# Laying the low parts of weights, x and activations 64 bytes further on in a decoder trunk

## The reference

```python
h = h + 0.5 * swiglu(rmsnorm(h, ln_ffn1[i]), ffn1_wi[i], ffn1_wo[i])   # d_ff = 2816
u = rmsnorm(h, ln_mix[i])
h = h + mixer(u)                     # layers 0 and 3: stick-breaking attention, 1: mLSTM, 2: latent attention
h = h + 0.5 * swiglu(rmsnorm(h, ln_ffn2[i]), ffn2_wi[i], ffn2_wo[i])
# swiglu(x, wi, wo): gate, up = split(x @ wi); (silu(gate) * up) @ wo
```

## Time and profile before

| | |
|---|---|
| time, median of 3 runs (lowest to highest) | 1944.04 us (1943.8 to 1944.66) |
| time of the profiled execution | 1943.6 us |
| its span, first to last instruction | 1941.9 us |
| its mean granted TensorE clock | 0.998 of full speed (2.4 GHz) |
| PE busy | 1922.5 us, 99% of the span, 10778 matmuls |
| PEld busy | 1657.6 us, 85% |
| DVE busy | 1367.0 us, 70% |
| ACT busy | 1128.4 us, 58% |
| DMA | 343.35 MB, mean 177 GB/s |

### The profile page before, as it was taken

The page is one execution under the profiler, slowest core; times in us unless marked ns, Lnnn a source line. Parts: engine busy times, 40 slices in busy tenths (PEclk is TensorE's granted clock), DMA queues, the critical chain, the costliest instruction groups (busy, mean ns, idle before and its releaser), DMA issues.

```text
span 1941.9 us, 29533 instructions
## 1 busy us (share of the span) xinstructions
PE 1922.5 (99%) x10778; PEld 1657.6 (85%) x10778; DVE 1367.0 (70%) x1844; ACT 1128.4 (58%) x1678; POOL 64.3 (3%) x138
## 2 busy tenths in 40 slices
PE   8999999999999999999999999999999999999998
PEld 6888988888888888888888889888888888978887
DVE  6766776767776686676777776676677776767666
ACT  6555575555655566655565555765555556556553
POOL 2000000000100000000010001000000000000000
PEclk9999999999999999999999999999999999999999
DMA  6555534655555553455655554355556555535553
GB/s 219 194 194 196 174 131 137 210 194 193 165 192 190 170 195 130 154 194 194 208 175 192 186 172 124 130 174 194 194 173 204 186 185 178 172 125 166 192 194 119
DMA packets 244095, 343.35 MB, mean 177 GB/s; under 512 B 12077, under 2 KB 196026, under 8 KB 244026
## 3 DMA queue, kind: packets, MB, share of 16 engines
q1 hardware_dynamic: 242016, 340.29, 53.1%
q10 hardware_dynamic: 2010, 2.12, 0.5%
HBM read 340.27 MB, written 1.05 MB: 176 GB/s over the span
## 4 chain that ended last, share of the span: by engine, by line
PE 95%; DVE 2%; ACT 1%; DMA 0%; issue 0%; SPq 0%; ACTq 0%; POOL 0%; POOLq 0%; DVEq 0%
PE psum L532 33%; PE psum L695 33%; PE psum L703 17%; PE psum L990 5%; PE psum L563 1%; PE psum L1634 1%; DVE wlo L494 1%; PE psum L1032 1%; ACT whi L475 0%; PE psum L1691 0%; DVE mix L1181 0%; DMA raw<-in_ffn_wi 0%; PE psum L1043 0%; PE psum L1721 0%; PE psum L1668 0%
## 5 line engine op out<-in xcount | busy, mean ns | idle before, releaser
L475 ACT ACTIVATE whi<-raw,gains 128x512 fp32r<-128x512 f32 (+2 forms) x876 | 557.1, 709 | 266.5 <-PE psum L703 192.7
L695 PE MATMUL psum<-xT,whi 128*128 128x512 f32 x2816 | 678.6, 392 | 2.3 <-DVE wlo L515 1.9
L494 DVE SCALAR_TENSOR_TENSOR wlo<-raw,gains,whi 128x512 fp32r<-128x512 f32 (+2 forms) x876 | 596.8, 743 | 57.5 <-ACT whi L475 57.5
L695 PEld LDWEIGHTS psum<-xT,whi 128*128 128x128 f32 x2816 | 522.5, 188 | 111.2 <-issue 4.8
L703 PEld LDWEIGHTS psum<-xT,wlo 128*128 128x128 f32 x2816 | 344.3, 189 | 6.8
L703 PE MATMUL psum<-xT,wlo 128*128 128x256 f32 x2816 | 346.3, 281 | 0.0
L811 DVE TENSOR_TENSOR gate_in_T<-psum,low 128x512 f32<-128x512 f32 x88 | 60.9, 692 | 337.8 <-ACT low L758 337.4
L490 DVE TENSOR_TENSOR wlo<-raw,whi 128x2048 fp32r<-128x2048 f32 x100 | 228.5, 2285 | 43.7 <-ACT whi L471 43.7
L532 PE MATMUL psum<-wlo,hidT_hi 128*128 128x512 f32 x640 | 251.4, 393 | 0.0
L532 PE MATMUL psum<-whi,hidT_hi 128*128 128x512 f32 x640 | 249.0, 389 | 0.0
L532 PE MATMUL psum<-whi,hidT_lo 128*128 128x512 f32 x640 | 248.6, 388 | 0.0
(11 more groups left out here) (230 smaller groups left out, 1534.5 us busy)
## 6 DMA issues: line engine op xcount, KB each, us to landing
raw<-in_ffn_wi SPq DMA_DIRECT2D x350, 512.0 KB, 4.6
raw<-in_ffn_wo SPq DMA_DIRECT2D x176, 512.0 KB, 4.3
raw<-in_sb_w_in SPq DMA_DIRECT2D x48, 512.0 KB, 4.5
raw<-in_ml_w_in SPq DMA_DIRECT2D x24, 512.0 KB, 4.4
raw<-in_sb_w_out SPq DMA_DIRECT2D x16, 512.0 KB, 4.0
raw<-in_ml_w_out SPq DMA_DIRECT2D x8, 512.0 KB, 4.0
raw<-in_mla_w_out SPq DMA_DIRECT2D x8, 512.0 KB, 4.3
raw<-in_mla_w_in SPq DMA_DIRECT2D x4, 512.0 KB, 4.5
```

Of the source, the lines that this page charges most:

```text
L475: last = act.activation(whi[:, slot, r], raw[:, slot, r], ACT.Copy, scale=gain_col(p.gain + k))
L494: last = dve.scalar_tensor_tensor(wlo[:, slot, p.at + r.start:p.at + r.stop], raw[:, slot, r], gain_col(p.gain + k), hi[:, r], op0=ALU.mul ...
L695: i = pe.matmul(psum[:, 4 + blk, :], whi[:, slot, k * 2 * FC + blk * P:k * 2 * FC + (blk + 1) * P], xT[:, 4 * part + k, :, :].rearrange("p ...
```

## The change

The diff moves tiles; no instruction is added or removed on any engine. Beside what is shown, only the order of declarations changes.

```diff
-                  for s in range(2)], at=SHIFT)
+                  for s in range(2)])
...
         whi = sb("whi", [P, RING, PCOLS], F32R)
-        wlo = sb("wlo", [P, RING, PCOLS + 32], F32R)
+        minus_half = sb("minus_half", [P, 16])
+        wlo = sb("wlo", [P, RING, PCOLS], F32R)
+        gains1 = sb("gains1", [P, N_GAINS_1])
         ssq = sb("ssq", [P, TT])
         mean_sq = sb("mean_sq", [P, TT])
...
         h = sb("h", [P, TT, D])
-        xT = sb("xT", [P, KD, 2, SEQ], F32R)
-        xT_hi, xT_lo = xT[:, :, 0, :], xT[:, :, 1, :]
+        hidT_hi = sb("hidT_hi", [P, FC // P, SEQ], F32R)
+        xT = sb("xT", [P, 2, KD * SEQ + 16], F32R)
+        xT_hi, xT_lo = (xT[:, a, 0:KD * SEQ].rearrange("p (k n) -> p k n", k=KD) for a in range(2))
+        gains2 = sb("gains2", [P, N_GAINS_2])
+        ident_b = sb("ident_b", [P, P], BF16)
+        hidT_lo = sb("hidT_lo", [P, FC // P, SEQ], F32R)
         hid = sb("hid", [P, 2, SEQ])
...
-                dve.tensor_tensor(wlo[:, slot, p.at:p.at + w], raw[:, slot, 0:w], hi[:, 0:w], ALU.subtract).then_inc(lo_ready, 1)
+                dve.tensor_tensor(wlo[:, slot, 0:w], raw[:, slot, 0:w], hi[:, 0:w], ALU.subtract).then_inc(lo_ready, 1)
...
-                i = pe.matmul(psum[:, 4 + blk, :], whi[:, slot, k * 2 * FC + blk * P:k * 2 * FC + (blk + 1) * P],
-                              xT[:, 4 * part + k, :, :].rearrange("p a n -> p (a n)"),
+                i = pe.matmul(psum[:, 4 + blk, :].rearrange("p (a n) -> p a n", a=2), whi[:, slot, k * 2 * FC + blk * P:k * 2 * FC + (blk + 1) * P],
+                              xT[:, :, (4 * part + k) * SEQ:(4 * part + k + 1) * SEQ],
...
-                i = pe.matmul(psum[:, 4 + blk, 0:SEQ], wlo[:, slot, SHIFT + k * 2 * FC + blk * P:SHIFT + k * 2 * FC + (blk + 1) * P],
+                i = pe.matmul(psum[:, 4 + blk, 0:SEQ], wlo[:, slot, k * 2 * FC + blk * P:k * 2 * FC + (blk + 1) * P],
```

More of the change, by code:

```diff
@@ L41 @@
 PCOLS = 2048
-SHIFT = 16
 MIX_COLS = 16704
@@ L88, with __init__ @@
 class Piece:
-    def __init__(self, tiles, cols, gain, sources, views=None, at=0):
+    def __init__(self, tiles, cols, gain, sources, views=None):
         self.tiles, self.cols, self.gain, self.sources, self.views = tiles, cols, gain, sources, views
-        self.at = at
 def rope_twice(raw, hi, lo):
@@ L150, in trunk @@
         whi = sb("whi", [P, RING, PCOLS], F32R)
-        wlo = sb("wlo", [P, RING, PCOLS + 32], F32R)
+        minus_half = sb("minus_half", [P, 16])
+        wlo = sb("wlo", [P, RING, PCOLS], F32R)
+        gains1 = sb("gains1", [P, N_GAINS_1])
         ssq = sb("ssq", [P, TT])
         mean_sq = sb("mean_sq", [P, TT])
-        rstd = sb("rstd", [P, TT])
-        pos_i = sb("pos_i", [P, TT], I32)
         h = sb("h", [P, TT, D])
-        xT = sb("xT", [P, KD, 2, SEQ], F32R)
-        xT_hi, xT_lo = xT[:, :, 0, :], xT[:, :, 1, :]
+        hidT_hi = sb("hidT_hi", [P, FC // P, SEQ], F32R)
[4 more added lines that the diff above has]
+        hidT_lo = sb("hidT_lo", [P, FC // P, SEQ], F32R)
         hid = sb("hid", [P, 2, SEQ])
@@ L162, in trunk @@
         gate_in_T = sb("gate_in_T", [P, 2, SEQ])
-        hidT_hi = sb("hidT_hi", [P, FC // P, SEQ], F32R)
-        hidT_lo = sb("hidT_lo", [P, FC // P, SEQ], F32R)
         y = sb("y", [P, TT, D])
-        gains1 = sb("gains1", [P, N_GAINS_1])
-        gains2 = sb("gains2", [P, N_GAINS_2])
         ident = sb("ident", [P, P])
-        ident_b = sb("ident_b", [P, P], BF16)
         tri_work = sb("tri_work", [P, 2, P])
@@ L178, in trunk @@
         mask = sb("mask", [P, 6, NCOL], BF16)
-        minus_half = sb("minus_half", [P, 16])
+        rstd = sb("rstd", [P, TT])
         gate_bias = sb("gate_bias", [ML_HEADS, 2])
+        pos_i = sb("pos_i", [P, TT], I32)
         mix = sb("mix", [P, MIX_COLS])
@@ L493, in convert_dve @@
                 r = slice(k * p.cols, (k + 1) * p.cols)
-                last = dve.scalar_tensor_tensor(wlo[:, slot, p.at + r.start:p.at + r.stop], raw[:, slot, r],
-                                                gain_col(p.gain + k), hi[:, r],
+                last = dve.scalar_tensor_tensor(wlo[:, slot, r], raw[:, slot, r], gain_col(p.gain + k), hi[:, r],
                                                 op0=ALU.mult, op1=ALU.subtract)
@@ L514, in first_dve @@
                 r = slice(k * p.cols, (k + 1) * p.cols)
-                dve.scalar_tensor_tensor(wlo[:, 0, p.at + r.start:p.at + r.stop], raw[:, 0, r], gain_col(p.gain + k),
-                                         whi[:, 0, r].bitcast(F32),
+                dve.scalar_tensor_tensor(wlo[:, 0, r], raw[:, 0, r], gain_col(p.gain + k), whi[:, 0, r].bitcast(F32),
                                          op0=ALU.mult, op1=ALU.subtract).then_inc(first_lo if k < p.tiles - 1 else lo_ready, 1)
```

## The result

The changed kernel takes 1963.84 us (median of 4 runs, 1961.63 to 1964.4) against 1944.0 before: ratio 1.0099, 95% interval 1.0086 to 1.0112. It is slower by 1%; the prediction was 1939.4 us, with 1951 as the upper end. The granted clock is 0.997 of full speed against 0.998; a thousandth of the span is 2 us, so the loss is not one of clock.

The account below looks back on a forecast made before the run. The prediction took PE's distance between matmul starts as the bound. Its terms −2.8 − 0.9 − 1.3 + 0.4 = −4.6 us took 1943.6 to 1939.0, or 1939.4 us for the median of runs; range 1927 to 1951.

Parts of the forecast that it names:

- What bounds the kernel: Whole kernel: PE, busy 99% of the span, sets the end by the distance between matmul starts; DVE and ACT are cover.
- rows 6 to 8: FFN and mLSTM timelines: streaming from slot 1, 128 bytes off the weights loaded beside it, costs 7.1 ns more a matmul.
- Step 4: `up_both`, 2816 matmuls: x low moved to 64 costs 0, since the next load reads during the first 256 columns; bounds +20, −39 us.
- rival b: `up_both`: reading x low 64 off, or the jump of 8256 bytes, costs, 234 ns each; 1959 us, chance 0.13.
- Step 1: `wlo` off the 128: −2.8 us in five FFNs' down matmuls, −0.9 us in eleven pieces with `xT` stationary.
- Rival c: Where `wlo` streams, low against low at 64 costs 7.1 ns: +3.6 − 0.9, so 1946.7 us; chance 0.08.
- Step 2: `turned_half`, 864 matmuls of 256 columns: two of three pairs come to lie 64 apart, −1.3 us; bounds 0 and −5.5.
- Step 3: Latent attention's own products: one pair in three loses its good place (113.6 ns), +0.4 us; bounds 0 and +1.5.
- Step 5: ACT and DVE: same counts at other places, hidden behind PE, 0; without that cover 35 us at the utmost.
- Rival a: PE matmuls: address means nothing, slot 1's 7 ns come from something that stays; 1944.0 us, chance 0.17.
- Rival d: `up_both` second half and `turned_half`: more comes back, as at the 113.6 ns seen in the trace; 1924 us, chance 0.15.

Follow-up runs that it names:

- ring_2112: Kernel before with a `wlo` ring stride of 2112 words, so its down pieces lie at 0 modulo 256 in every slot; 1942.89 us (0.9992).
- wlo_2064: Kernel before with a `wlo` ring stride of 2064 words: down pieces at 64 in slot 1, at 128 in slot 2; 1951.79 us.
- x_split_64: Kernel before with x alone stored as in the change: two blocks, low half at 64 modulo 256; 1959.38 us (1.0076).
- x_hi_64: Kernel before with x in two blocks, high half at 64 and low at 0, low-weight ring at 0 (stride 2048 words); 1961.58 us.
- x_split_0: Kernel before with x in two blocks, but the low block at 0 modulo 256; 1944.16 us (1.0002).
- sweep_whi: Kernel before, low-weight ring at 0 (stride 2048 words), `whi` of the up pieces 32 bytes further on in each successive FFN; 1959.75 us.
- low_64: Kernel before with the change's other half, without x: low weights of all pieces and `hidT_lo` 64 bytes off; 1951.89 us (1.0043).
- hidT_64: ring_2112 with both `hidT_hi` and `hidT_lo` at 64, so all down matmuls have one distance; 1956.04 us.
- shift_48: ring_2112 with the low weights of the up products 192 bytes off modulo 256 in all slots; 1943.36 us (0.9997).

## Why the prediction was wrong

*What bounds the kernel* held: PE alone sets the end, and no wait appeared. So did the reading of rows 6 to 8 that slot 1 costs by its address (ring_2112, wlo_2064).

*Step 4, `up_both` at 0,* is the step that failed: it set the remainder of x low at nothing, and +16.0 us were measured, 5.7 ns on each of 2816. The step's upper bound, +20, held it, and rival b's 1959 us, with a chance of 0.13, came nearest. The argument that only the first 256 columns meet the next weight load was wrong: x_split_64 pays with the second half at 64, x_hi_64 with the first. Rows 12 spoke for the jump alone, and rightly (x_split_0); the price of the remainder rested on that argument. Of rival b's two reasons the remainder is the one; by sweep_whi, if only differences count, more by its change within one stream than by the distance of the half that moved.

*Step 1, −2.8 and −0.9,* came out +4.4 and +2.6, so it failed as well. What the address of slot 1 cost was right. The reading that the stream counts against the weights loaded beside it was not enough: it made all differences 0, and low_64, where they are 0, takes 5.537 us for 24 down matmuls in place of 5.440. The change ends one kind of matmul in three that stood 128 off in five FFNs, and in all eight sets two kinds of three off their own weights, at 192 and 64, with the remainder changing from matmul to matmul. How much of the loss is distance and how much is the changing stays open. Rows 11, both operands at 64, could not tell: there the streamed operand lies 0 from its own weights and from the next, which `wlo` over `hidT_hi` does not. Rival c put +3.6 in step 1's place (measured +7.0), but for `wlo` alone, where all three kinds pay.

*Step 2, −1.3,* came out: `turned_half` measured −1.1. By either pairing two of its three kinds lie off after the change, so it does not tell the pairings apart. The timeline after, seven triples as in rows 9:

```profile
202.34 0.28 PE L986 MATMUL psum<-xT,wlo 128*128 128x256 f32 x1
...
204.82 0.28 PE L986 MATMUL psum<-xT,wlo 128*128 128x256 f32 x1
```

2.48 us against 2.52. (The 2.47 that the prediction gave as the sign is 117.8 ns for all 21; its own two thirds make 2.49.) *Step 3, +0.4,* measured +0.9, within its bounds, but not by one kind in three: in a run of 36 the matmuls stand 118.0 ns apart on average, where they stood at 113.6. *Step 5, 0,* held. Not forecast were −1.5 in `up_rest` and −1.1 in the transposes.

Rival a is refuted: x_split_64 and x_split_0 hold the same instructions and data, and one remainder makes 1959.38 − 1944.16 = 15 us. The sentence of the Trainium skill that the prediction set beside it ("SBUF — State Buffer", Who interferes with whom: "PE and ACT never wait on anyone"), read as the prediction read it, that an address costs PE nothing, disagrees with these 15 us. Whether the loss is a wait at a port no run here shows. Rival d's hope was real in kind: 113.3 ns exists for `up_rest`, at an address that this change does not use.

## What to carry to other kernels

Where PE is busy throughout and matmuls stand a few per cent above their columns, compare the addresses of the stationary and of the streamed operand modulo 256, and measure a sweep of that distance in one kernel, one value per stage, before trusting an argument about it. Keep one remainder within a stream and from one matmul to the next where you can: a mixture of two distances can cost more than the shares of both (5.559 us for 24 in wlo_2064, where the shares make 5.493 at most). The best distance differs by shape: here 512 columns wanted 0 and 256 columns wanted 88. A row that clears one cause of a cost (the jump) says nothing on another that comes with it (the remainder).

## What the runs showed of the hardware

In cycles of the full clock, 2.4 GHz, the settled spacings are whole multiples of 16: 226.7 ns is 544 (512 columns and 32 more), 113.3 ns is 272 (256 and 16), 120.0 ns is 288 (256 and 32), and 233.3 ns, where x_hi_64's `up_both` settles, is 560. In hidT_64, at a distance of 64, 233.3 is only a mean: single spacings alternate between 231 and 236 ns. 117.8 ns, which `up_rest` also holds through whole runs, is no such multiple. At the lower level of the clock this surplus is not there: in the kernel before, in a stretch granted 1.2 GHz, after a run of one-column matmuls (L1616) and four of 256 columns, twelve products of the latent attention take 1192.17 − 1189.61 = 2.56 us, 213.3 ns each, which is 256 cycles for 256 columns.

Which spacing a run settles in depends on the distance and on more. In x_split_64 `up_rest` settled at 113.3 ns in the three FFNs whose pieces lay at 64 and 192; in the kernel before, the same FFNs at the same distances, behind faster `up_both`, took 117.8. The latent attention stands at 113.6 ns with distance 192, `up_rest` with 192 at 117.8 (shift_48). Why 88 bytes gives 272 cycles and 80 or 96 do not, stays open; no run lies between them. Open too is when a change of distance from one matmul to the next costs by itself. In the kernel before, slot 1 has one kind of three at distance 128 and takes 5.494 us, as the mean (5.440 + 5.440 + 5.589)/3 = 5.490 would; with one kind of three at 192, wlo_2064 takes 5.559, where the mean would be 5.458.
